# One inference step of a hybrid decoder layer: v as seven block products, one turned buffer, and another order of VectorE's and GpSimd's work around a chunk's norm

## The chip, the cores and the metric

The kernel runs on one core of one Trainium2 chip. The metric is the device time of one execution, in microseconds; the time before is the median of three runs. Everything is float32. Engines are named as in the profile: PE is TensorE, DVE VectorE, ACT ScalarE, POOL GpSimd, SP SyncE, which here only issues DMAs.

## What is computed

One decoder layer for a prompt of 2048 tokens and for 8 sample sequences of 4 tokens, model width 1024.

```python
h = rms_norm(x, norm1_g) * (1 + scale1) + shift1        # shift, scale, gate: silu(c) @ w_ada + b_ada
q, k, v, u, vg = split(h @ w_in)                        # each 512 wide
q, k = rms_norm per head                                # 8 heads of 64
o_sb = stick_breaking(q, k, v)                          # samples: with 8192 past tokens of a paged cache
u = gelu(u); vn = rms_norm(gelu(vg)) per group          # 4 groups of 128
o_mlp = u * (causal w_s @ vn + b_s)                     # in chunks of 128 tokens
x = x + gate1 * (concat(o_sb, o_mlp) @ w_out)
h2 = rms_norm(x, norm2_g) * (1 + scale2) + shift2
up = h2 @ w_up                                          # 5632 wide, then a causal width-3 convolution
x = x + gate2 * ((silu(g_ff) * v_ff) @ w_down)
```

k, v, the samples' vn and the last rows of up are outputs too.

## The kernel before

The program has four stages, each with one instruction list per engine. The engines meet at semaphores alone.

**Preparation** (`prepare`) makes constants and the first third of the conditioning vectors.

**Input projection** (`project_in`) works on pairs of 128-token tiles, 8 pairs, and on one group of the 32 sample rows between pair 6 and pair 7. For u, g, q and k a pair's product [256 x 1024] x [1024 x 512] is split into 2 x 2 blocks and worked as seven block products instead of eight. Their names are 1, 2, 6, 5, 7, 3 and 4; each is four tiles of 128 rows against 256 columns. The differences of weight blocks (`tdiff`) are made once by DVE, and one of them replaces its block in place; the sums of token blocks (`sums`) are made once a pair by POOL. Products 1, 6, 5 and 4 are copied out of PSUM by ACT, 2, 7 and 3 are added by DVE. v is two plain products, one for each tile of tokens: 8 tiles against 512 columns each (line 619). The order of all events is one list, `in_events`, written by hand, which every engine walks through; `with_conditioning` puts into it the steps of the other two thirds of the conditioning product: 16 steps, each one 1024 KB piece of `w_ada` into `ada` and four groups of matmuls with 512 columns side by side (line 650), behind product 5 of u, g, q and k in pairs 1 to 4. Transposed q and k go through the buffer `turned`, the gate's output through `omT`, each copied by ACT (`copy`) and stored by SP. SP issues in the order of the events and waits there, so everything behind a waiting SP instruction waits too.

**Attention of the prompt** (`attend_prompt`) is not changed, but for one small load that is issued in its span, the page table.

**The rest** (`finish_layer`) works on four chunks of 512 tokens, the last with the 32 sample rows. A chunk is a list of units: 4 of the output projection (OUT), 22 of the up projection (UP), 12 of the down projection (DOWN). A unit is again seven block products, in the order 1, (4 of the unit before), 2, 6, 5, 7, 3; the first two UP units are interleaved: 1 1 2 2 5 5 6 3 7 6 4 3 7. Product 6 waits until 1 has been taken out of PSUM, 5 for 2, 7 for 6, 3 for 5 and 4 for 7. POOL makes the sums of a unit's weight blocks one unit ahead (`weight_sums`), DVE the differences of the moving operand (`difference`). Product 5 of an UP unit needs the first difference. The last DOWN unit of a chunk is carried into the next chunk: it stands between that chunk's OUT units and its UP units and covers the norm. The norm: squares (the last four by DVE, line 2124), their sum by PE with a matrix of ones (line 1864), root by ACT, reciprocal by DVE, scaling by DVE and POOL (lines 2169, 2238), modulation by ACT (line 1940), then the four differences for UP (line 2070). In chunk 0 nothing is carried, so the norm has no cover there.

Beside the units runs the attention of the samples over the cache, 64 steps, 23, 22 and 19 of them in chunks 0, 1 and 2. A step is four pieces: SCORE (PE, line 1376; then two sigmoids by ACT), WEIGH (a scan and a product by DVE, lines 1458 and 1462), MOVE (PE transposes, line 1382, and a DVE copy) and SUM (PE, line 1390). Each step needs 8 pages of keys and 8 of values, 256 KB each, that SP loads in order (lines 1334, 1337): the next step's keys when SCORE is done, its values when SUM is done; keys and values have one buffer each. `stage_plan` spreads the pieces: it adds up 1.75 us for each product of a full unit (three quarters of that for the third group of DOWN, nothing for the first two units), places a piece when its share of the chunk's total is due and two products have passed since the last piece, and holds SCORE back from the last OUT unit to the first UP product. In the last 20 us of a chunk's planned cost the two products are not asked for. Before, the first three WEIGHs in chunk 0's UP units stand behind products 31, 39 and 48 of its 258.

Of the kernel before, what the change touches and what calls it, by code (L numbers as in the profile page):

```python
# [12 lines left out]
P = 128  # L13
# [238 lines left out]
def constants(nc, ctx):  # L252

    def sb(name, shape, dt=F32):
# [7 lines left out]
        "bias": sb("bias", [P, 2, H]), "bias_s": sb("bias_s", [P, 2]), "pt": sb("pt", [1, NSEQ * NPAGE], I32),  # L262
# [15 lines left out]
LATE = 2 + NSEQ + 4 * TS  # L278
# [3 lines left out]
def in_events():  # L282
# [7 lines left out]
    for p in groups:  # L290
# [13 lines left out]
        else:  # L304
# [3 lines left out]
        events += [m("u", 1), m("u", 2), *late[0], *once(("tdiff", "g"), m("g", 1), m("g", 2)), m("u", 6), m("u", 5), *late[1], *once(("nsq", SAMPLE, 0)),  # L308
                   m("u", 7), *late[2], m("u", 3)]
        later = lambda *extra: list(extra) if p else []  # L310
        events += [*later(m("g", 1)), m("u", 4), ("gelu", p, "u"), *once(("stat", SAMPLE, 0), ("root", SAMPLE)), *later(m("g", 2)),
# [5 lines left out]
        events += [m("k", 1), m("q", 4), m("k", 2), m("k", 6), ("square", p, "q"), ("reduce", p, "q"), m("k", 5), ("hroot", p, "q"),  # L317
                   m("k", 7), ("hnorm", p, "q"), ("mix", p), *ahead(("modulate",)), m("k", 3), ("om", p)]
        events += [m("v", 0), ("turn", p, "om"), ("copy", p, "om"), *ahead(("sums",)), m("k", 4), ("square", p, "k"), ("reduce", p, "k"), ("turn", p, "q"),
                   ("hroot", p, "k"), ("copy", p, "q"), ("hnorm", p, "k"), ("gain", p, "k"), m("v", 1)]  # L320
# [13 lines left out]

def with_conditioning(events):
# [3 lines left out]
    for event in events:  # L339
# [3 lines left out]
        b = 1 + (n - 1) // KT  # L343
# [7 lines left out]
        if event[1] in range(1, 5) and event[2] in "ugqk" and event[3] == 5:  # L351
            placed.append(("mod", 1 + n // KT, n % KT))
            n += 1
            if n % KT == 0:
                placed.append(("mrow", n // KT))
                since = 0
# [11 lines left out]
def in_bank(p, kind, part):  # L368

    second = part in (2, 5, 3) or (kind == "v" and part == 1)  # L370
    return 2 * (IN_UNITS.index((p, kind)) % 2) + second
# [27 lines left out]
COPIES = [event[1:] + (t,) for event in IN_EVENTS if event[0] == "copy" for t in range(1 if event[1] == SAMPLE else 2)]  # L399
COPY_AT = {turn: n + 1 for n, turn in enumerate(COPIES)}  # L400
# [9 lines left out]
def project_in(nc, sem, a, k, nxt, dr, out):  # L410

    with ExitStack() as ctx:
# [5 lines left out]
        tw = {kind: sb("t_" + kind, [P, 3, halfk, HC]) for kind in "ugqk"}  # L418
        ss = sb("sums", [P, 4, halfk, P])
# [3 lines left out]
        turned, omT = sb("turned", [P, HP, 2 * P]), sb("omT", [P, G, 2 * P])  # L423
# [4 lines left out]
        cT, ada = nxt["cT"], sb("ada", [P, 2 * D])  # L428
# [75 lines left out]
        def _(sp):  # L504
# [21 lines left out]
            def store_cols(use, p):  # L526
# [3 lines left out]
                src, o, first = {"q": (turned, "qT", 0), "k": (turned, "kT", 0), "om": (omT, "catT", DSB)}[use]  # L530
# [4 lines left out]
            def load_ada(b, kt):  # L535
                if kt:
                    sp.wait_ge(mod_done, KT * (b - 1) + kt)
                elif b > 1:
                    sp.wait_ge(mod_turned, b - 1)
                src = a["w_ada"][0].rearrange("(t p) n -> t p n", p=P)[kt][:, 2 * D * b:2 * D * b + 2 * D]  # L540
                sp.dma_start(ada[:], src).then_inc(ada_loaded, 16)
# [14 lines left out]
            late(k["pt"][:], a["page_table"].rearrange("(a b) n -> a (b n)", a=1))  # L556
            for b in range(NSEQ):
                sp.dma_start(k["wd"][TS * b:TS * b + TS, :, TS * b:TS * b + TS], k["wsT"][0:TS, :, 0:TS]).then_inc(nxt["wd_loaded"], 16)
            for event in IN_EVENTS:
                name, *which = event  # L560
                if name == "mul" and which[1:] in (["v", 1], ["g", "s"]):
                    p, kind, part = which
                    if part == 1 and p + 2 < NPAIR:
                        sp.wait_ge(prod_done, prod((p, "v", 1)))
                        load_x(p + 2)
                    sp.wait_ge(taken, IN_TAKEN.index((p, kind, part)) + 1)
# [9 lines left out]
                if name == "mod" and which[1] + 1 < KT:  # L576
# [7 lines left out]
        def _(pe):  # L584
            def multiply(p, kind, part):
# [7 lines left out]
                if part == "s":  # L593
# [5 lines left out]
                    for n, (half, kt) in enumerate(left + right):  # L599
                        first, final = n in (0, KT), n in (KT - 1, KT + len(right) - 1)  # L600
                        into = slice(HC, DSB) if n >= KT else slice(0, HC)
                        for one in many:
                            if one == "v" and n >= KT and half == 0:
                                continue
# [1742 lines left out]
```

## Time and profile before

| | us |
|---|---|
| median of three runs | 3282.31 (3274.2 to 3282.68) |
| the profiled execution's own time | 3281.88 |
| its span | 3280.2 |
| PE busy | 3200.4 |
| DVE, POOL, ACT busy | 1628.4, 1573.4, 1154.9 |

The span is the time from the first instruction to the last in the profiled execution. In a row of the timeline the first number is the start in us from the span's start, the second the time that the merged instructions lasted; a bracket at the end gives the idle time before them and what ended it. The end of a matmul is modelled, so durations of PE are best read from start to start. The input projection lies between about 50 and 585 us, the prompt's attention ends at 1101, and chunks 1, 2 and 3 begin near 1670, 2225 and 2765.

### The profile page before, as it was taken

The page shows a single profiled execution, that of the slowest core. Times are in us where ns is not written, and L with a number is a line of the kernel's source. Part 1 is how long each engine was busy: PE and PEld are TensorE (multiplying, and loading weights), DVE is VectorE, ACT ScalarE, POOL GpSimd, SP SyncE. Part 2 cuts the span into 40 slices and gives each one's busy share as a digit, 9 for nine tenths or more (in the row PEclk, how much of TensorE's full clock was granted, in tenths as well). Part 3 has the DMA queues.
Part 4 walks back from the last instruction along what each step waited for, and adds up shares of the span by engine and source line. Part 5 has one row for each costly group of instructions (what it writes and reads, how often), then busy time and mean ns, then how long its engine had stood idle before and what let it go on. Part 6 is the DMA issues. An engine that isn't in the chain of part 4 may idle for free.

```text
span 3280.2 us, 53057 instructions
## 1 busy us (share of the span) xinstructions
PE 3200.4 (98%) x18534; PEld 2426.1 (74%) x18535; DVE 1628.4 (50%) x2326; ACT 1154.9 (35%) x2436; POOL 1573.4 (48%) x1287
## 2 busy tenths in 40 slices
PE   7999999899999999999999999999999999999999
PEld 5777786666666677777777777777777778788887
DVE  4222222388888554535435544544553445555455
ACT  3333333399999433212103322211331220242221
POOL 2322222176666555545445544544554444476563
PEclk8999999999999999999999999999999999999999
DMA  7233311321312467777886776777777765222222
GB/s 279 84 108 105 109 59 35 81 67 33 69 37 45 161 205 259 244 257 256 280 296 229 241 240 228 251 269 248 251 245 228 245 208 159 68 90 84 84 77 84
DMA packets 260882, 540.93 MB, mean 165 GB/s; under 512 B 45199, under 2 KB 82943, under 8 KB 240137
## 3 DMA queue, kind: packets, MB, share of 16 engines
q1 hardware_dynamic: 225464, 359.31, 34.7%
q10 hardware_dynamic: 35153, 178.23, 15.5%
q8 instruction: 149, 2.44, 0.3%
q14 instruction: 116, 0.95, 0.1%
HBM read 502.90 MB, written 34.55 MB: 164 GB/s over the span
## 4 chain that ended last, share of the span: by engine, by line
PE 60%; DVE 3%; issue 1%; SPq 1%; ACT 0%; DMA 0%; POOL 0%; DVEq 0%; POOLq 0%; ACTq 0%
PE ff_pB L1856 52%; PE s_pZ L1376 4%; PE s_pO L1390 4%; DVE ff_conv L2157 1%; DVE s_left L1458 1%; PE s_pZ L1382 0%; SPq L1326 0%; DVE ff_x L2094 0%; ACT ff_conv L1954 0%; PE s_pZ L1864 0%; DVE ff_raw L2143 0%; SPq L1337 0%; DVE s_stop L1462 0%; DVE ff_act_in L2070 0%; SPq L1334 0%
## 5 line engine op out<-in xcount | busy, mean ns | idle before, releaser
L1856 PE MATMUL ff_pB<-ff_act_in,ff_w 128*128 128x256 f32 (+1 forms) x2496 | 608.5, 388 | 13.4 <-DVE ff_act_in L2070 8.0
L1856 PEld LDWEIGHTS ff_pB<-ff_act_in,ff_w 128*128 128x128 f32 x2496 | 471.9, 192 | 114.3 <-issue 28.8
L2213 POOL TENSOR_TENSOR ff_sums<-ff_w 128x512 f32<-128x512 f32 (+1 forms) x152 | 192.5, 1266 | 729.5 <-PE ff_pB L1856 684.5
L2157 DVE SCALAR_TENSOR_TENSOR ff_conv<-ff_raw,k_vecT,ff_conv 128x512 f32<-128x512 f32 (+1 forms) x352 | 419.1, 1191 | 111.6 <-ACT ff_raw L1961 105.3
L2094 DVE SCALAR_TENSOR_TENSOR ff_x<-ff_pB,k_mod,ff_x 128x256 f32<-128x256 f32 (+2 forms) x448 | 213.9, 479 | 370.6 <-PE ff_pB L1856 368.8
L1856 PE MATMUL ff_pB<-ff_diff_up,ff_sums 128*128 128x256 f32 (+1 forms) x1600 | 388.2, 385 | 2.1 <-DVE ff_x L2094 1.3
L1987 ACT ACTIVATE ff_raw<-ff_pB 128x256 f32<-128x256 f32 (+1 forms) x352 | 135.9, 387 | 720.4 <-PE ff_pB L1856 703.0
L1268 POOL TENSOR_TENSOR at_stop<-at_stop,at_left 128x512 f32<-128x512 f32 (+2 forms) x320 | 314.7, 999 | 151.6 <-ACT at_stop L1203 76.7
L2143 DVE TENSOR_TENSOR ff_raw<-ff_raw,ff_pB 128x256 f32<-128x256 f32 (+1 forms) x264 | 112.0, 425 | 507.6 <-PE ff_pB L1856 507.5
L1856 PEld LDWEIGHTS ff_pB<-ff_diff_up,ff_sums 128*128 128x128 f32 x1600 | 301.2, 190 | 63.5 <-issue 13.6
L1252 DVE TENSOR_TENSOR_SCAN at_left<-at_go,at_left,at_one 128x512 f32<-128x512 f32 x192 | 235.3, 1267 | 47.5 <-ACT at_go L1203 45.2
L1856 PE MATMUL ff_pB<-ff_hidden,ff_w 128*128 128x256 f32 (+1 forms) x1056 | 258.4, 386 | 0.2
L2225 POOL TENSOR_TENSOR ff_raw<-ff_raw,ff_conv 128x512 f32<-128x512 f32 (+1 forms) x88 | 121.1, 1376 | 249.0 <-ACT ff_raw L1967 131.2
L1856 PEld LDWEIGHTS ff_pB<-ff_hidden,ff_w 128*128 128x128 f32 x1056 | 199.2, 191 | 41.1 <-issue 7.9
L2218 POOL TENSOR_TENSOR ff_sums<-ff_w,ff_sums 128x512 f32<-128x512 f32 (+1 forms) x152 | 218.5, 1437 | 11.9
L2216 POOL TENSOR_TENSOR ff_sums<-ff_w 128x512 f32<-128x512 f32 (+1 forms) x152 | 217.9, 1434 | 11.9
L1954 ACT ACTIVATE ff_conv<-ff_raw,k_vecT 128x512 f32<-128x512 f32 (+1 forms) x176 | 145.9, 829 | 209.6 <-DVE ff_raw L2143 207.5
L2214 POOL TENSOR_TENSOR ff_w<-ff_w 128x512 f32<-128x512 f32 (+1 forms) x152 | 206.2, 1356 | 0.0
L1856 PE MATMUL ff_pB<-ff_act_in,ff_sums 128*128 128x256 f32 (+1 forms) x832 | 200.7, 384 | 0.0
L1856 PE MATMUL ff_pB<-ff_diff_down,ff_sums 128*128 128x256 f32 (+1 forms) x768 | 189.3, 390 | 8.3 <-DVE ff_x L2094 7.8
L1856 PE MATMUL ff_pB<-ff_diff_up,ff_w 128*128 128x256 f32 (+1 forms) x800 | 194.1, 385 | 0.0
L1856 PEld LDWEIGHTS ff_pB<-ff_act_in,ff_sums 128*128 128x128 f32 x832 | 156.6, 190 | 31.7 <-issue 8.3
(249 smaller groups left out, 4917.4 us busy)
## 6 DMA issues: line engine op xcount, KB each, us to landing
ff_w<-in_w_units ACTq DMA_DIRECT2D x135, 1024.0 KB, 6.1
s_kpage<-in_cache_k SPq DMA_DIRECT2D x512, 256.0 KB, 3.9
s_vpage<-in_cache_v SPq DMA_DIRECT2D x512, 256.0 KB, 3.3
in_ada<-in_w_ada SPq DMA_DIRECT2D x16, 1024.0 KB, 4.9
ff_w<-in_w_units ACTq DMA_DIRECT2D x16, 768.0 KB, 4.4
in_w<-in_w_in SPq DMA_DIRECT2D x5, 2048.0 KB, 20.7
in_hT<-in_x_cols SPq DMA_DIRECT2D x8, 1024.0 KB, 6.9
wada<-in_w_ada SPq DMA_DIRECT2D x3, 2048.0 KB, 15.5
```

The costliest lines, as they stand in the source:

```text
L1252: dve.tensor_tensor_scan(left[:, e, x0:x1][:, ::-1], go[:, s % RS, e, c0:c1][:, ::-1], other, first, ALU.mult, ALU.bypass).then_inc(left_r ...
L1268: pool.tensor_tensor(w, w, left[:, e, x0 + 1:x1 + 1], ALU.mult).then_inc(w_ready, 1)
L1376: last = pe.matmul(self.pZ[g][32 * sl:32 * sl + 32, 0:ZC].rearrange("p (j t) -> p j t", j=PG), self.q[:, SG * g + sl, hp, :], self.kpage[: ...
L1856: last = pe.matmul(into, left[:, kt * P:(kt + 1) * P], right[:, kt, :], start=kt == 0 and p in (1, 2, 5), stop=kt == depth(n) - 1, skip_gr ...
L1954: act.activation(conv[:, f % 2, half, 0:taps_width(c)], raw[:, f % 2, half, 2:2 + taps_width(c)], ACT.Identity, scale=k["vecT"][:, 196 + f ...
L1987: act.activation(dst, C if p == 5 else A, ACT.Copy).then_inc(taken, 1)
L2094: dve.scalar_tensor_tensor(into, bank[:, 0:hi - lo], mod, into, ALU.mult, ALU.add).then_inc(added, 1)
L2157: dve.scalar_tensor_tensor(cv, raw[:, f % 2, half, i:i + taps_width(c)], tap, cv, ALU.mult, ALU.add).then_inc(tapped, 1)
L2213: pool.tensor_tensor(S3, A11, A21, ALU.subtract).then_inc(sums_ready, 1)
L2214: pool.tensor_tensor(A21, A21, A22, ALU.add).then_inc(sums_ready, 1)
L2216: pool.tensor_tensor(S2, A21, A11, ALU.subtract).then_inc(sums_ready, 1)
L2218: pool.tensor_tensor(S4, A12, S2, ALU.subtract).then_inc(sums_ready, 1)
```

## The change

In the input projection:

- v becomes seven block products like the others, with its own `tdiff` in pair 0; the sample rows add the block that was replaced in place. The order of a pair's events changes: g's products 1 and 2 always stand between u's 2 and 6, v's products are mixed with k's end, and `sums` of the next pair stands behind v's product 7. S1 is made in place of A21, which saves a quarter of `sums`.
- `omT` goes; all copies use `turned`, and each waits for the store of the copy before.
- `ada` is half as large. The conditioning product becomes 32 steps of 512 KB and 256 columns, behind product 5 of all five kinds from pair 1 on.
- The page table's tile moves out of the constants and is loaded among the sample attention's inputs.

In the rest:

- In a chunk with a carried unit, POOL waits for all squares of the norm before it makes the weight sums of the first UP unit. The second half of the sum of squares comes behind the carried unit's product 2 instead of 1.
- The first difference for UP stands behind the second UP unit's product 1 instead of the first UP unit's product 2.
- The samples' scaling in chunk 3 (`scale_sample`) goes from DVE to POOL.
- The planner places a WEIGH only behind a product 7 or 3, and not behind those of the first UP unit, as long as more than 20 us of the chunk's planned cost are left. In chunks 1 and 2 SCORE is held back until the first UP unit's product 5.

```diff
-LATE = 2 + NSEQ + 4 * TS
+LATE = 1 + NSEQ + 4 * TS
...
-        events += [m("v", 0), ("turn", p, "om"), ("copy", p, "om"), *ahead(("sums",)), m("k", 4), ("square", p, "k"), ("reduce", p, "k"), ("turn", p, "q"),
-                   ("hroot", p, "k"), ("copy", p, "q"), ("hnorm", p, "k"), ("gain", p, "k"), m("v", 1)]
+        events += [m("v", 1), m("k", 4), m("v", 2), ("turn", p, "om"), ("copy", p, "om"), ("square", p, "k"), ("reduce", p, "k"), m("v", 6),
+                   ("hroot", p, "k"), m("v", 5), ("hnorm", p, "k"), ("turn", p, "q"), ("copy", p, "q"), ("gain", p, "k"), m("v", 7),
+                   *ahead(("sums",)), m("v", 3), m("v", 4)]
...
+ADA_STEPS = 2 * KT
...
-        if event[1] in range(1, 5) and event[2] in "ugqk" and event[3] == 5:
-            placed.append(("mod", 1 + n // KT, n % KT))
+        if event[1] in range(1, NPAIR) and event[3] == 5 and n < 2 * ADA_STEPS:
+            placed.append(("mod", 1 + n // ADA_STEPS, n % ADA_STEPS))
...
-                        last = pe.matmul(pM[32 * n:32 * n + 32, :], cT[:, kt, :], ada[:, 512 * n:512 * n + 512], start=kt == 0, stop=kt == KT - 1)
+                        last = pe.matmul(pM[32 * n:32 * n + 32, into], cT[:, kt, :], ada[:, 256 * n:256 * n + 256], start=kt == 0, stop=kt == KT - 1)
...
+                    if COPIED_BEFORE[p, use]:
+                        q, other = COPIED_BEFORE[p, use]
+                        act.wait_ge(stored[other], stores(q))
...
-                        pool.wait_ge(prod_done, prod((p - 1, "k", 3)))
-                    pool.tensor_tensor(S1, A21, A22, ALU.add).then_inc(sums_ready, 1)
+                        pool.wait_ge(prod_done, prod((p - 1, "v", 7)))
                     pool.tensor_tensor(S3, A11, A21, ALU.subtract).then_inc(sums_ready, 1)
+                    pool.tensor_tensor(A21, A21, A22, ALU.add).then_inc(sums_ready, 1)
...
-        marks[carried, 1] = roots + [("invert", 0)]
-        marks[carried, 2] = scale(0, 0)
+        marks[carried, 1] = roots[0] + [("invert", 0)]
+        marks[carried, 2] = roots[1] + scale(0, 0)
...
-    for i, place in enumerate(((up, 2), (up + 1, 2), (up, 5), (up + 1, 5))):
+    for i, place in enumerate(((up + 1, 1), (up + 1, 2), (up, 5), (up + 1, 5))):
...
-        if event == ("mul", up, 1):
+        if event == ("mul", up, 5 if c else 1):
             held = False
...
-            if (held and pieces[placed][1] == SCORE) or (since < 2 and total - spent > 20):
+            piece = pieces[placed][1]
+            if (held and piece == SCORE) or (since < 2 and total - spent > 20):
+                break
+            if piece == WEIGH and total - spent > 20 and (event[0] != "mul" or event[2] not in (7, 3) or event[1:] in ((up, 3), (up, 7))):
                 break
...
+                if is_carried(n):
+                    pool.wait_ge(squared_dve, 4 * c + 8)
                 if n + 1 < NU:
                     weight_sums(n + 1)
                 if is_carried(n):
                     scale(c + 1)
```

## Rows read from the trace of the kernel before

**Rows 1.** Busy time and share of TensorE over the span, from the page.
```profile
PE 3200.4 (98%) x18534; PEld 2426.1 (74%) x18535; DVE 1628.4 (50%) x2326; ACT 1154.9 (35%) x2436; POOL 1573.4 (48%) x1287
```

**Rows 2.** Waits of TensorE by what ended them: us in total, times, longest.
```profile
PE ff_pB L1856 <- DVE ff_x L2094: 10.2, 14, 2.2
PE ff_pB L1856 <- DVE ff_act_in L2070: 8.0, 4, 2.9
...
PE s_pZ L1864 <- DVE ff_hidden L2124: 6.1, 4, 3.5
...
PE s_pZ L1376 <- DMA s_kpage<-in_cache_k: 1.9, 2, 1.1
```

**Rows 3.** Timeline of one v product (16 matmuls) and what follows: start, duration, instruction.
```profile
314.20 7.03 PE L619 MATMUL in_pB<-in_w,in_hT 128*128 128x512 f32 x16
...
321.06 1.04 PE L695 MATMUL in_pX<-k_ident,in_raw_u 128*128 128x128 f32 x8
```

**Rows 4.** Timeline of TensorE around one conditioning step in pair 1.
```profile
159.61 1.89 PE L628 MATMUL in_pB<-in_t_k,in_sums 128*128 128x256 f32 x8
161.34 1.89 PE L628 MATMUL in_pB<-in_w,in_sums 128*128 128x256 f32 x8
163.16 1.06 PE L650 MATMUL in_pM<-in_ada,in_cT 128*32 128x512 f32 x8
...
165.98 1.95 PE L678 MATMUL in_pX<-in_raw_g,k_wsT 128*128 128x128 f32 x16
```

**Rows 5.** Timeline of the sample rows' turn of k and its copy.
```profile
574.57 0.43 PE L695 MATMUL in_pX<-k_ident,in_raw_k 32*128 32x32 f32 x4
...
575.39 0.28 ACT L827 ACTIVATE in_turned<-in_pX 128x128 f32<-128x128 f32 x1 [2.03 <-DMA scratch_qT<-in_turned]
```

**Rows 6.** Timeline of TensorE at chunk 0's first product 5 of UP.
```profile
1184.11 3.35 PE L1856 MATMUL ff_pB<-ff_act_in,ff_w 128*128 128x256 f32 x8 [2.16 <-DVE ff_act_in L2070]
...
1187.25 0.63 PE L1382 MATMUL s_pZ<-k_ident,s_stop 128*128 128x128 f32 x2
```

**Rows 7.** Timeline of POOL, DVE and TensorE around chunk 1's norm.
```profile
1727.72 1.27 POOL L2213 TENSOR_TENSOR ff_sums<-ff_w 128x512 f32<-128x512 f32 x1 [6.91 <-PE ff_pB L1856]
1728.13 2.55 DVE L2124 TENSOR_TENSOR ff_hidden<-ff_x 128x256 f32<-128x256 f32 x2
...
1730.73 1.13 PE L1864 MATMUL s_pZ<-ff_hidden,k_ones 128*128 128x256 f32 x4 [1.00 <-DVE ff_hidden L2124]
...
1750.31 1.99 PE L1856 MATMUL ff_pB<-ff_act_in,ff_w 128*128 128x256 f32 x8 [1.49 <-DVE ff_act_in L2070]
```

**Rows 8.** Timeline of TensorE around chunk 3's norm.
```profile
2830.65 2.18 PE L1864 MATMUL s_pZ<-ff_hidden,k_ones 128*128 128x272 f32 x4 [3.54 <-DVE ff_hidden L2124]
...
2832.62 2.77 PE L1856 MATMUL ff_pB<-ff_hidden,ff_w 128*128 128x256 f32 x6
...
2837.20 1.46 PE L1856 MATMUL ff_pB<-ff_hidden,ff_w 128*128 128x256 f32 x6
...
2852.78 5.62 PE L1856 MATMUL ff_pB<-ff_act_in,ff_w 128*128 128x272 f32 x16 [2.91 <-DVE ff_act_in L2070]
```

**Rows 9.** Timeline of TensorE at the first of the long waits on ff_x.
```profile
1385.34 3.20 PE L1856 MATMUL ff_pB<-ff_diff_down,ff_sums 128*128 128x256 f32 x8 [2.10 <-DVE ff_x L2094]
```

**Rows 10.** Timeline of SP's page loads and of two SCOREs, chunks 1 and 2.
```profile
1758.04 9.00 SPq L1337 DMA_DIRECT2D s_vpage<-in_cache_v  x8
...
1780.75 1.93 PE L1376 MATMUL s_pZ<-s_kpage,s_q 128*32 128x256 f32 x32 [1.12 <-DMA s_kpage<-in_cache_k]
...
2315.41 8.38 SPq L1337 DMA_DIRECT2D s_vpage<-in_cache_v  x8
...
2336.93 1.29 PE L1376 MATMUL s_pZ<-s_kpage,s_q 128*32 128x256 f32 x20
```

**Rows 11.** DMA issues: count, KB each, median us from issue to landing.
```profile
s_kpage<-in_cache_k SPq DMA_DIRECT2D x512, 256.0 KB, 3.9
s_vpage<-in_cache_v SPq DMA_DIRECT2D x512, 256.0 KB, 3.3
```

## What was predicted before the run

> **What bounds the kernel now.** I read the busy table first: TensorE works 3200.4 of 3280.2 us [rows 1], so time comes off only by giving it less work or by taking its few waits away. A wait costs it more than its length: after an idle stretch its matmuls run at half pace for some time. Then the waits of TensorE, by what ended them [rows 2]: VectorE's work on the residual tile ff_x (10.2 us), on the operand differences of the up projection (8.0), on the squares of a chunk's norm (6.1); a page of cached keys ended two (1.9). Then the timeline around each place that the diff touches. Everything else that the diff edits lies on engines that wait for TensorE.
>
> **Input projection, v.** A product of 4 tiles of 256 columns starts 1.73 us before the next (159.61 to 161.34) [rows 4]. A v product of before, 8 tiles of 512 columns, takes 6.86 us (314.20 to 321.06) [rows 3], and a pair has two, 13.72. Seven block products take 7 x 1.73 = 12.1. That is 1.62 us less, in 8 pairs: -13.0.
> Beside it: the four subtractions for v stand once, on VectorE in pair 0, where it is mostly idle. ScalarE copies four small blocks and VectorE adds three instead of two large copies. GpSimd's sums for the next pair now start after v's product 7 and have v's 3 and 4, u's 1 and 2, the turn of k and g's 1 and 2 before their first user, six products or 10.4 us, for three operations that last 1.3 us each; that is what moving g's two products ahead covers. I cost all of these at nothing; one miss on TensorE would cost 1 to 3 us in each pair.
>
> **The conditioning product in 32 halves.** It sits between two products: 161.34 to 165.98 is 4.64 us, two products are 3.45, so one step costs 1.19 us [rows 4]. Its two passes of 512 columns take 2 x 0.429 (6.86 us / 16 matmuls), four groups side by side; the other 0.33 us is the change over. With 256 columns: 0.43 + 0.33 = 0.76. 32 x 0.76 - 16 x 1.19 = +5.3. The ends are 0 (cost halves with the columns) and +19 (cost stays); I take +5.3. The loads are half as large and the closest two steps are 5 products apart.
>
> **One turned buffer.** Each copy now waits for the store of the copy before. For a full pair some 4 us of products lie between om's copy and q's, and more before k's. For the sample rows they follow at once: before, the copy of k waited 2.03 us for q's store and stood at 575.39, while TensorE's turn of k was at 574.57 [rows 5]. Now om's copy waits for that store, and the turn of k needs om's bank back: 575.4 + 0.3 - 574.6 = +1.1. The page table's load moves behind other loads; nothing needs it for 500 us.
> Input projection: -13.0 + 5.3 + 1.1 = -6.6.
>
> **The norms, one per chunk.** Chunk 0: VectorE's first difference stood behind a sample step's scan and VectorE's add, TensorE idled 2.16 us and the next product took 3.14 instead of 1.73 (1184.11 to 1187.25) [rows 6]. Now the difference is one product earlier and the scan (WEIGH) can't stand in the block: 2.16 + 1.41 = -3.6. The idle time ahead of the block, which waits for the norm itself, stays.
> Chunks 1 and 2: two squares took 2.55 us (1728.13) [rows 7], where one alone takes 0.42, beside GpSimd's weight sums of 1.27 us each. Now GpSimd waits for all squares and the second half's sum comes one product later: the wait of 1.00 goes, and a wait of 0.4 behind it. The wait for the difference, 1.49, shrinks to about 0.4, since the scores and the scan leave, but the modulated tiles come no sooner. -2.4 each, -4.8.
> Chunk 3: 3.54 us of waiting, 1.1 in the slow sum and, from 2832.62 to 2837.20, 4.58 us for what takes 2.6 [rows 8]: 6.6. At the difference 2.91 idle, and 5.62 for two products that at 1.83 and a tail of 0.16 take 3.8: 4.7. The three sample operations leave VectorE for GpSimd and end about when ScalarE's last modulation does; I leave 0.5. -10.8.
> On the slow squares the Trainium skill, "SBUF — State Buffer", section "Who interferes with whom", says that GpSimd and a VectorE operation with two SBUF inputs exclude each other for a whole instruction. By that rule the trace agrees (1.27 us a square beside sums of 1.27 us), and it speaks against the change too: GpSimd's later sums meet the differences.
> GpSimd's next sums end 0.5 to 1.5 us later than before; they are needed three products on. Norms: -19.2.
>
> **WEIGH only behind products 7 and 3.** Of the 14 waits on ff_x [rows 2], 11 with 8.3 us fall where sample steps run, the longest with a scan ahead of the add that product 5 needs, and then the product takes 3.20 instead of 1.89 [rows 9]; that happens twice. 8.3 + 2.6 = 10.9 at most. Behind 3 the scan meets the taps, so I take -9.
>
> **What the rule costs.** The planner spreads pieces by time and asks for two products between them. A step is SCORE, WEIGH, MOVE, SUM. In a unit the order is 1, 4, 2, 6, 5, 7, 3. When the planner is late, a WEIGH behind 7 is followed by MOVE +2, SUM +4, SCORE +6 and WEIGH +8, behind the next unit's 3; from a 3, +8 is forbidden and the next is +13. So two steps cost at least 21 products, 10.5 each. Chunk 0 has 418.25 us of planned cost for 23 steps, or 10.4 products each: it can't catch up. Its first WEIGH in the block of up units moves from product 31 to 40, and the next ones, worked on, are at 48, 61, 69, 82 and so on to 237. At product 243 the remaining cost falls to 19.7 and the rule lapses (it holds above 20); 84 pieces are placed and 87.7 are due, so SCORE, WEIGH, MOVE and SUM of one step stand at one place. Chunks 1 and 2 need only 11.8 and 12.1 products a step and catch up near products 240 and 200.
> The bunch: let S be the start of the SUM before it, two small products (2.6 us) and that SUM (1.9) earlier than the SCORE. Its values are issued at S+2.1, in 8 to 9 us (1758.04) [rows 10], and land 3.3 later [rows 11]: S+13.5. Without waiting TensorE would be there at S+6.6, after SCORE and MOVE: +7. The next keys are issued after the values: S+2.1+8.2+0.8+8.2+3.9 = S+23.2, and that SCORE would be reached at S+18 to 19: +4.5. Half pace after both: +2.5. Together +14. Ends: +5 (only the scan's latency) and +19.
> Late steps also crowd the pages. 25 times (9 in chunk 0, 9, 7) a SCORE is 10 products behind the SUM that lets SP start on 16 page loads. Before this spacing occurs three times: 1.12 us of waiting (1780.75) [rows 10], 0.8, and none (2336.93) [rows 10]. In the last 21.5 us lie between the first issue (2315.41) and the SCORE; needed are two sets of issues of 8.2 to 9 each, 0.8 between them and 3.9 to land [rows 11], 21.1 to 22.7. 25 x 0.35 = +9; ends 0 and +28.
>
> **The sum.** -6.6 - 19.2 - 9 + 14 + 9 = -11.8 on the profiled execution's own 3281.88 us, 3270.1; the median of before is 0.4 above it: 3270.5.
>
> **Rivals.**
> A, the gains without the crowding: SP's loads land in time everywhere and the bunch costs its scan's latency alone (+5). Speaks for it: the loads take 0.74 to 0.77 of the DMA engines, not all, and the case in chunk 2 has no wait. Against: two of three waited. 3282.3 - 34.8 + 5 = 3252.5.
> B, the other side: pages become the bound. Each late SCORE waits the 1.12 us of the longer case (+28), and the bunch costs +19, against gains of 34.8: +12, 3294.5. It decides against the change from 0.64 us a place on, with a bunch of 19, which is just the mean of the three waits; for 1.12 speaks that both waits fell where a weight load ran beside, against it that after a step of 13 products SP has nothing left over.
> C, GpSimd becomes late at the norms and in the differences: its sums of 1.3 us, held back until the squares are done, meet VectorE's four differences in each of four blocks and hold product 5 or 6 by 1.3 to 2.5 us with half pace behind. The norms then give 8 instead of 19: 3281. For it: GpSimd has no idle time in the block; against: its sums are needed later than the differences. The lock of the skill's page gives the same, with each difference 1.3 us later.
>
> **Numbers.** Forecast 0.45 (its own range 3262 to 3280), A 0.2, B 0.1, C 0.2, the rest 0.05. The range is 3250 to 3289. About 0.3%, 9.8 us, is what a measurement can tell from no change, so faster means below 3272.5. Of the forecast 0.6 lies below, all of A, nothing of B, 0.15 of C: faster 0.5. Slower, above 3292: 0.09. The same: 0.41.
>
> **What would show it.** Matmuls into in_pB with 512 columns gone, v's products 1.73 apart, and the conditioning matmuls 64 x 4 with 256 columns, no waits of TensorE among them: right. The stretch to the end of the input projection shorter by 6 to 7 us. Waits on ff_hidden's squares near 0.5 us in total, on differences below 1.5. Waits of s_pZ for s_kpage of some 13 us, over 20 times, and one for s_vpage of over 2 near the end of chunk 0, with MOVE directly behind SCORE. If neither is there, A holds; if keys wait over 25 us, B; if the sums stand as releasers of product 5 or 6, C. A new wait in the input projection would refute my zeros there.

## The result, and the profile after

| | before | after |
|---|---|---|
| median of 6 runs, us | 3282.49 (3274.2 to 3284.04) | 3299.05 (3295.49 to 3305.3) |
| span of the profiled execution | 3280.2 | 3303.3 |

The ratio is 1.0061 with a 95% interval of 1.005 to 1.0072: slower by 0.6%, which is more than the 0.3% that a measurement can tell from no change. "After" is the changed kernel. The forecast was 3270.5 (range 3250 to 3289, 0.09 for slower). It was wrong in sign.

From the profile of after, its busy line and the chain of work that ended last. In before that chain was 60% PE and 1% SPq, SP's own instructions:

```profile
PE 3197.2 (97%) x18862; PEld 2465.7 (75%) x18863; DVE 1648.0 (50%) x2351; ACT 1156.4 (35%) x2452; POOL 1593.9 (48%) x1290
...
PE 47%; SPq 8%; DVE 4%; issue 4%; DMA 3%; ACT 1%; POOL 0%; DVEq 0%; ACTq 0%; POOLq 0%
```

PE works 3 us less than in [rows 1] and the span is 23 us longer, so some 26 us of new idle time stand somewhere. The waits of PE in after, by what ended them, in the form of [rows 2] (us in total, times, longest):

```profile
PE s_pZ L1375 <- DMA s_kpage<-in_cache_k: 22.2, 19, 2.4
PE s_pO L1389 <- DVE s_wT L1465: 13.7, 11, 2.9
PE ff_pB L1859 <- DVE ff_x L2097: 11.5, 17, 1.7
...
PE s_pO L1389 <- DMA s_vpage<-in_cache_v: 4.3, 1, 4.3
...
PE in_pX L696 <- ACT in_turned L822: 3.2, 1, 3.2
...
PE s_pZ L1867 <- DVE ff_hidden L2127: 0.5, 1, 0.5
```

Keys were expected (some 13 us, over 20 times), the one wait for values of over 2 too, and the squares at 0.5. Two lines were not: SUM waits 13.7 us for s_wT, the copy of the moved weights, and ff_x has as much as in [rows 2] where I had taken 9 us off.

To see where the time lies I cut each trace at the first matmul of a norm's sum of squares (us; a stage runs from one chunk's norm to the next, the last to the end of the span):

| kernel | chunk 0's norm to 1's | to 2's | to 3's | to the end |
|---|---|---|---|---|
| before | 562.4 | 557.4 | 539.7 | 460.0 |
| after | 588.9 | 563.2 | 542.9 | 450.7 |
| norms_alone | 557.5 | 554.9 | 538.1 | 450.4 |
| no_rule | 557.1 | 554.9 | 538.1 | 450.7 |
| half_pages | 579.1 | 558.2 | 540.7 | 450.7 |
| move_act | 583.8 | 558.9 | 539.2 | 450.7 |
| half_move | 570.8 | 555.1 | 536.6 | 450.7 |
| late_only | 557.0 | 566.0 | 542.7 | 450.7 |

The last column, where no sample step runs, has most of the gain that was worked out (9.3 of 10.8). The loss stands where sample steps run, most of it in chunk 0. The other kernels of the table are the experiments.

### The profile page after: what moved, and what is told of

Its sections match the earlier page's. It is cut to its first block, busy times and chain, and to the rows that moved or that the text cites. A ratio compares the mean times of both kernels' runs of the same rounds, so it can differ in the third digit from the quotient of the medians.

```text
span 3303.3 us, 53814 instructions
## 1 busy us (share of the span) xinstructions
PE 3197.2 (97%) x18862; PEld 2465.7 (75%) x18863; DVE 1648.0 (50%) x2351; ACT 1156.4 (35%) x2452; POOL 1593.9 (48%) x1290
## 4 chain that ended last, share of the span: by engine, by line
PE 47%; SPq 8%; DVE 4%; issue 4%; DMA 3%; ACT 1%; POOL 0%; DVEq 0%; ACTq 0%; POOLq 0%
PE ff_pB L1859 41%; SPq L1325 4%; DMA s_kpage<-in_cache_k 3%; PE s_pO L1389 3%; PE s_pZ L1375 3%; DVE ff_conv L2160 2%; SPq L1336 2%; SPq L1333 2%; ACT ff_conv L1957 1%; DVE ff_act_in L2172 0%; DVE ff_x L2097 0%; DVE s_left L1457 0%; DVE ff_raw L2146 0%; DVE ff_diff_down L2073 0%; PE s_pZ L1867 0%
## 5 line engine op out<-in xcount | busy, mean ns | idle before, releaser
L1859 PEld LDWEIGHTS ff_pB<-ff_act_in,ff_w 128*128 128x128 f32 x2496 | 471.7, 191 | 96.6 <-issue 22.2
L628 PE MATMUL in_pB<-in_w,in_hT 128*128 128x256 f32 x960 | 229.7, 386 | 6.0 <-ACT in_hT L782 6.0
L2204 POOL TENSOR_TENSOR ff_w<-ff_w 128x512 f32<-128x512 f32 (+1 forms) x152 | 216.1, 1422 | 0.0
L628 PEld LDWEIGHTS in_pB<-in_w,in_hT 128*128 128x128 f32 x960 | 185.4, 194 | 32.9 <-issue 6.6
```

The costliest lines, as they stand in the source:

```text
L628: last = pe.matmul(bank[:, 0:HC], left[:, kt, :], right[:, kt, :], start=kt == 0 and part in (1, 2, 5), stop=kt == halfk - 1, skip_group_c ...
L1859: last = pe.matmul(into, left[:, kt * P:(kt + 1) * P], right[:, kt, :], start=kt == 0 and p in (1, 2, 5), stop=kt == depth(n) - 1, skip_gr ...
L2204: pool.tensor_tensor(A21, A21, A22, ALU.add).then_inc(sums_ready, 1)
```

## The experiments

All times are medians. The kernel before ran beside each on the same chip, and the ratio is to that. Kernels of different tables are best compared by their ratios.

### One part of the change at a time

**input_alone** takes the input projection (and the page table's move), **norms_alone** the other order around the norm, **rule_alone** the planner's rule on WEIGH. Each is the kernel before with the lines of the change for that part. **no_rule** is the changed kernel without the rule:

```diff
-            if piece == WEIGH and total - spent > 20 and (event[0] != "mul" or event[2] not in (7, 3) or event[1:] in ((up, 3), (up, 7))):
-                break
```

> The kernel before with the input projection of the changed one (v as seven products, conditioning in halves, one turned buffer, the page table's move) and nothing else of the change. Theory (the two traces: the first product of the last stage starts 2.1 us earlier, since 7.6 us are gained up to the sample rows and most of it is lost again around their stores): 2 us less than before, about 3280.5. Rival (the working of the prediction): 6.6 us less, 3276. Second rival: the input projection is what made the changed kernel slower, by something its own trace hides behind the later stages; then over 3290.

> The kernel before with only the other order around a chunk's norm (GpSimd waits for all squares, the second half's root one product later, the first difference one product earlier, scores held back to product 5, the sample rows' scaling on GpSimd). Theory (chunk 3's norm took 9.3 us less in the changed kernel's trace, chunk 0's block 3 to 4, chunks 1 and 2 about 1 to 2.4 each): 14 to 19 us less than before, about 3266. Rival (GpSimd's later weight sums meet VectorE's differences and hold products 5 or 6): 8 us or less, 3275 or more.

> The kernel before with only the planner's rule that a WEIGH stands behind a product 7 or 3. Theory (the rule makes steps late in each chunk; pages of keys, the SUM behind VectorE's copy of the moved weights, and the bunch at the end of chunk 0 then hold TensorE): 30 to 36 us more than before, about 3315, with over 15 waits on s_kpage. Rival (the rule costs no more than it saves, and what slowed the changed kernel is the input projection's or the norms'): 3274 to 3290.

> The changed kernel without the planner's rule on WEIGH, all else kept. Theory: the rule alone made it slower, so this one is faster than both, 3262 to 3268, with fewer than 5 waits on s_kpage and the waits of SUM on s_wT gone. Rival (pages wait for another reason, such as the input projection's or the norms' shift): 3295 to 3300, the waits on s_kpage stay.

| kernel | us | ratio | 95% interval |
|---|---|---|---|
| before, in the same runs | 3280.54 | | |
| input_alone | 3276.87 | 0.9987 | 0.9978 to 0.9996 |
| norms_alone | 3263.52 | 0.9946 | 0.9932 to 0.9959 |
| rule_alone | 3311.10 | 1.0090 | 1.0077 to 1.0104 |
| no_rule | 3263.31 | 0.9941 | 0.9928 to 0.9955 |

The rule alone costs 30.6 us on before, and in the changed kernel 0.0120 of 3281, 39 us. It is the whole of the loss: without it the changed kernel is 17 us faster than before. Part of the 9 us between the two prices is that on before the rule also does some of the norms' work: rule_alone's waits on the first differences are 3.7 us where before has 8.0 [rows 2]. The norms give 17.0; norms_alone's stages in the table are shorter than before's by 4.9, 2.5, 1.6 and 9.6, together 18.5. The input projection gives 3.7 with an interval of 1.3 to 7.2, so the 2.1 of the two traces and the 6.6 of the prediction both lie in it, and this run doesn't decide between them.

The waits of rule_alone and, below it, of no_rule, which has none of a SCORE on s_kpage and none of a SUM of the steps on s_wT. Those two lines come with the rule and go with it. The rule takes nothing from ff_x in total: the two longest waits there, 2.10 and 2.19 us, are gone in after, and three of 1.67 have come.

```profile
PE s_pZ L1376 <- DMA s_kpage<-in_cache_k: 19.3, 17, 2.2
PE s_pO L1390 <- DVE s_wT L1466: 11.5, 11, 2.9
PE ff_pB L1859 <- DVE ff_x L2097: 10.6, 15, 1.7
```

```profile
PE ff_pB L1857 <- DVE ff_x L2095: 11.3, 16, 2.2
...
PE s_pZ L1381 <- DVE s_stop L1461: 4.5, 6, 0.9
```

### What the rule's price is made of

**half_pages** loads half of each page and lets it stand in for the other half, so that it leaves out half of the cached keys and values but keeps TensorE's work; **move_act** moves one copy from VectorE to ScalarE, **half_move** does both, all in the changed kernel.

```diff
-                sp.dma_start(self.kpage[:, j, sl, :], src).then_inc(self.k_loaded, 16)
+                sp.dma_start(self.kpage[:, j, sl, 0:DSB // 2], src[:, 0:DSB // 2]).then_inc(self.k_loaded, 16)
```

```diff
 def act_piece(self, act, N, i):
...
+        if i == MOVE:
+            act.wait_ge(self.wT_done, N + 3)
+            act.activation(self.wT[:].rearrange("p j q -> p (j q)"), self.pZ[g][:, ZC:ZC + PG * P], ACT.Copy).then_inc(self.wT_read, 1)
...
 def dve_piece(self, dve, N, i):
...
-        if i == MOVE:
-            dve.wait_ge(self.wT_done, N + 3)
-            self.dve_move(dve, slice(0, P), PG, g)
```

> The changed kernel with page loads of half the size: of each cached page only the first 256 of 512 columns are loaded and stand in for the other 256 too (so half of the cached keys and values is left out), TensorE's matmuls keep their number and size. Theory (late steps let SP's page loads, bound by their data, end the waits: 22.2 us on keys and 4.3 on values in the changed kernel's trace, plus some half pace behind them): 22 to 30 us less, 3269 to 3277, no waits on s_kpage, the 13.7 us of SUM on s_wT stay. Rival (SP's own work of issuing, not the data, sets the pace): eight loads still take over 6 us to issue, over 10 us of waits on s_kpage stay, over 3285.

> The changed kernel with the copy of the moved weights (s_wT) on ScalarE instead of VectorE, so that it doesn't queue behind VectorE's taps. Theory: the 11 waits of SUM, 13.7 us, go, with some half pace behind them: 14 to 18 us less, 3281 to 3285. Rival (pages set the pace of the steps whatever SUM does): the waits on s_kpage grow by as much and the time stays over 3293.

> Both edits, half-size page loads and the copy on ScalarE, in the changed kernel. Theory (pages and the late copy are all that the planner's rule costs): 3255 to 3263, at or below the kernel without the rule (3263.3); below it if the rule does take away collisions of the scan with the adds. Rival (a further cost of late steps that neither edit touches): over 3268.

| kernel | us | ratio | 95% interval |
|---|---|---|---|
| before, in the same runs | 3280.97 | | |
| half_pages | 3285.34 | 1.0014 | 1.0005 to 1.0023 |
| move_act | 3289.76 | 1.0025 | 1.0015 to 1.0034 |
| half_move | 3273.68 | 0.9976 | 0.9967 to 0.9985 |

Against the changed kernel's ratio the three are 15, 12 and 28 us faster. All three forecasts missed: I had 22 to 30 for half_pages, which came out at its rival's edge, 14 to 18 for move_act, and half_move at or below no_rule, where it stays 11 us above by the ratios.

move_act's waits show that the two causes hang together, and that the copy was not freed altogether:

```profile
PE s_pZ L1375 <- DMA s_kpage<-in_cache_k: 15.3, 16, 3.0
PE ff_pB L1859 <- DVE ff_x L2097: 13.9, 21, 1.7
...
PE s_pO L1389 <- ACT s_wT L1422: 5.6, 4, 1.8
```

SUM's wait falls from 13.7 to 5.6 us, the waits for keys fall with it by 6.9, although no load was changed, and ff_x rises by 2.4. A SUM that is late delays the loads behind it. So the price of the late copy and that of the pages can't be added up singly.

The stages say where the rest lies. Of the 45 us by which after's first three stages are longer than no_rule's, the two edits together take 32.5. In chunks 1 and 2 half_move is within 0.2 of no_rule and 1.5 below it; the two waits are all that the rule costs there. In chunk 0 it stays 13.8 above. Laid against no_rule matmul by matmul, it is 1.8 us ahead at 1620 us, 13.8 behind at 1654 and 13.8 behind at the chunk's end. So what is left arises in that one place, near the end of chunk 0, where SCORE, WEIGH, MOVE and SUM of one step stand behind one product. The matmuls of PE there, start, duration, what it idled for:

```profile
1637.87 0.44 PE L1381 MATMUL s_pZ<-k_ident,s_stop 128*128 128x128 f32 x2 [1.91 <-DVE s_stop L1465]
1643.43 3.64 PE L1390 MATMUL s_pO<-s_vpage,s_wT 128*32 128x512 f32 x16 [5.13 <-DMA s_vpage<-in_cache_v]
```

The same place in the changed kernel, with SP's loads:

```profile
1646.54 1.92 PE L1389 MATMUL s_pO<-s_vpage,s_wT 128*32 128x512 f32 x16
...
1648.72 8.40 SPq L1336 DMA_DIRECT2D s_vpage<-in_cache_v  x8
...
1652.81 1.93 PE L1375 MATMUL s_pZ<-s_kpage,s_q 128*32 128x256 f32 x32 [1.56 <-DMA s_kpage<-in_cache_k]
...
1656.64 0.44 PE L1381 MATMUL s_pZ<-k_ident,s_stop 128*128 128x128 f32 x2 [1.90 <-DVE s_stop L1461]
...
1661.35 3.64 PE L1389 MATMUL s_pO<-s_vpage,s_wT 128*32 128x512 f32 x16 [4.27 <-DMA s_vpage<-in_cache_v]
1664.92 2.50 PE L1859 MATMUL ff_pB<-ff_hidden,ff_sums 128*128 128x256 f32 x6
```

With S = 1646.54 the values are issued at S+2.2 and the SUM starts at S+14.8; the prediction had S+2.1 and S+13.5. Idle 1.56, 1.90 and 4.27, then 1.7 and 1.0 of half pace, and 0.35 and 1.21 at the next two SCOREs (1669.07 and 1693.43): 12.0, where I had put 14. Three of these waits, 3.1 us, are among the 22.2 us for keys. No run takes the bunch away by itself.

half_pages also shows what paces the page loads. The timeline of SP in half_pages, one set of keys and one of values:

```profile
1209.52 8.39 SPq L1333 DMA_DIRECT2D s_kpage<-in_cache_k  x8
1219.00 8.15 SPq L1336 DMA_DIRECT2D s_vpage<-in_cache_v  x8
```

and in the changed kernel:

```profile
1211.50 8.40 SPq L1333 DMA_DIRECT2D s_kpage<-in_cache_k  x8
1220.71 8.04 SPq L1336 DMA_DIRECT2D s_vpage<-in_cache_v  x8
```

The DMA issues (KB each, median us from issue to landing) of half_pages and then of the changed kernel, where [rows 11] had 3.9:

```profile
s_kpage<-in_cache_k SPq DMA_DIRECT2D x512, 128.0 KB, 2.6
```

```profile
s_kpage<-in_cache_k SPq DMA_DIRECT2D x512, 256.0 KB, 4.6
```

Half the bytes leave the eight issues at 8.0 to 8.4 us. The bytes don't set that pace, as the rival said; SP's own instructions fill most of it. What fell is the landing, by 2.0 us, and since the mean wait on keys was 22.2 / 19 = 1.17, that was enough: of 22.2 us 2.9 stayed, in one wait behind the bunch. So the rival was right about the pace, and the theory about the waits. By the instructions of the address lookup, from the trace of the changed kernel (duration min/median/max in ns), a load takes 269 + 152 ns ahead of its issue, which itself takes 338; from one load to the next it is 1.1 us:

```profile
L1325 SPq TENSOR_LOAD <-k_pt x32: 262/269/287, 1202.8 to 1237.9; - x32
L1325 SPq FUSED_REGOPS  x32: 152/152/159, 1203.1 to 1238.5; - x32
```

**late_only** keeps the rule in chunks 1 and 2 alone:

```diff
-            if piece == WEIGH and total - spent > 20 and (event[0] != "mul" ...
+            if c and piece == WEIGH and total - spent > 20 and (event[0] != "mul" ...
```

> The changed kernel with the planner's rule on WEIGH in chunks 1 and 2 only; chunk 0 is planned without it. Theory (chunk 0, whose steps can't catch up and end in the bunch, pays 32 of the rule's 45 us in the traces, chunk 1 8 and chunk 2 5): 10 to 16 us above the kernel without the rule, 3272 to 3279. Rival (chunks 1 and 2 catch up as chunk 0 can't, and their waits are the run's own spread): within 4 us of 3263.

It took 3274.51 us (before 3280.37), ratio 0.998, interval 0.997 to 0.9989: 11 us above no_rule by the medians and 13 by the ratios, as the theory had it. Chunk 0 is back at 557.0. So chunk 0 pays about 32 of the rule's 45 us in the traces, by the table. Chunk 1 is 2.8 us longer here than in after (566.0 against 563.2) under the same rule; why, I did not find.

### The sample rows' stores

**no_rule_cols** is no_rule with three separate places in the one turned buffer for the 32 sample rows:

```diff
+SAMPLE_COLUMN = {"q": 0, "om": S, "k": 2 * S}
...
-                    if COPIED_BEFORE[p, use]:
+                    at = SAMPLE_COLUMN[use] if p == SAMPLE else 0
+                    if at == 0 and COPIED_BEFORE[p, use]:
...
-                        into = dst[:, :, t * R:(t + 1) * R]
+                        into = dst[:, :, at + t * R:at + (t + 1) * R]
```

> The changed kernel without the planner's rule, and with the three stores of the sample rows' turned tiles taken from columns of their own (0, 32 and 64) of the one turned buffer, so that their copies don't wait for one another's stores. Theory (the copy of om waited 4.3 us for a store queued behind a conditioning load; TensorE then idled 2.7 to 3.2 us and ran at half pace for some 3 more): 4 to 6 us less than without the columns, 3257 to 3260, the wait on in_turned gone. Rival (TensorE's turns wait for something else in its place, or the store of q then holds the conditioning step): 3261 to 3265.

It took 3256.47 us, ratio 0.9920 (0.9907 to 0.9934): 6.8 us less than no_rule, a little more than the 4 to 6 of the theory. What it took away, in the changed kernel:

```profile
569.66 0.40 SPq L547 DMA_DIRECT2D in_ada<-in_w_ada  x1
...
570.47 0.38 SPq L537 DMA_DIRECT2D scratch_qT<-in_turned  x1
574.72 0.28 ACT L822 ACTIVATE in_turned<-in_pX 128x128 f32<-128x128 f32 x1 [4.28 <-DMA scratch_qT<-in_turned]
...
575.14 0.60 PE L696 MATMUL in_pX<-k_ident,in_raw_k 32*128 32x32 f32 x4 [3.24 <-ACT in_turned L822]
575.67 3.78 PE L628 MATMUL in_pB<-in_w,in_sums 128*128 128x256 f32 x8
```

and in no_rule_cols:

```profile
571.25 0.43 PE L698 MATMUL in_pX<-k_ident,in_raw_k 32*128 32x32 f32 x4
571.61 1.99 PE L630 MATMUL in_pB<-in_w,in_sums 128*128 128x256 f32 x8
```

The store of q took 4.2 us to land where it had taken 2.2 before. SP had issued a 512 KB conditioning load 0.8 us ahead of it, which itself took 4.7. That the load is the cause is read from this order; no run moves the load alone, and no_rule_cols takes away the wait and not the slow landing. The Trainium skill, "DMA: Bandwidth & Descriptors", section "Queues, rings and completion order", says that each DMA engine works off the descriptors of one issuing engine in ring order; by that rule the trace agrees, the store landing 0.35 us behind the load.

### Two gentler rules

**narrow** is no_rule_cols with a WEIGH forbidden only behind product 6; **narrow3** adds a third product between WEIGH and MOVE in chunks 1 and 2; **move3** has only that.

```diff
+            if piece == WEIGH and total - spent > 20 and event[0] == "mul" and event[2] == 6:
+                break
+            if piece == MOVE and c and since < 3:
+                break
```

> The changed kernel with columns of their own for the sample rows' stores, and in place of the rule on WEIGH a narrow one: no WEIGH directly behind a product 6, the only place where a scan ran into the add that product 5's successor needs for over 2 us (twice, with under 1 us in other places). Theory: the steps keep their spacing, two waits of 2.1 and 2.2 us on ff_x go, with some slow matmuls behind: 3 to 6 us less than with the columns alone (3256.5), so 3250 to 3253. Rival (a WEIGH one product later meets the taps, and the wait only moves to SUM or MOVE): 3255 to 3258.

> As the kernel with the narrow rule, and in chunks 1 and 2 a MOVE stands at least three products behind its WEIGH instead of two. Theory (MOVE waited five times 0.8 to 0.9 us for the weights in the trace without the rule): 3 to 5 us less than the narrow rule alone. Rival (each step's SUM comes a product later, and the pages of keys after it become late, as under the full rule): no gain, or up to 5 us more, with waits on s_kpage.

> As no_rule_cols (no rule on WEIGH, columns of their own for the sample rows), and in chunks 1 and 2 a MOVE stands at least three products behind its WEIGH; the narrow rule of the run before is left out. Theory (the gain of that run over the narrow rule came from MOVE no longer waiting behind the taps and the scan, and the narrow rule itself gave nothing): 3250 to 3254, no waits on s_stop in chunks 1 and 2. Rival (both are needed, since only a WEIGH off product 6 avoids the two long waits on ff_x): 3255 to 3260.

| kernel | us | before beside it | ratio | 95% interval |
|---|---|---|---|---|
| narrow | 3265.06 | 3280.37 | 0.9956 | 0.9943 to 0.9970 |
| narrow3 | 3252.14 | 3280.37 | 0.9912 | 0.9899 to 0.9926 |
| move3 | 3257.13 | 3281.22 | 0.9924 | 0.9911 to 0.9938 |

narrow was a miss of 12 us or more, on the side of its rival and beyond it. Its stages are 2.4 and 3.3 us longer than no_rule_cols's in chunks 1 and 2. Its trace has MOVE waiting 3.73 us, in chunk 1 and again in chunk 2, because the scan, one product later, came behind the taps and ran at 1.85 us instead of 0.75, beside a GpSimd operation (1764.08, 1.26 us):

```profile
1760.42 3.51 DVE L2163 SCALAR_TENSOR_TENSOR ff_conv<-ff_raw,k_vecT,ff_conv 128x512 f32<-128x512 f32 x2
...
1764.03 1.85 DVE L1460 TENSOR_TENSOR_SCAN s_left<-s_go,s_left 128x256 f32<-128x256 f32 x1
...
1767.11 0.44 PE L1384 MATMUL s_pZ<-k_ident,s_stop 128*128 128x128 f32 x2 [3.73 <-DVE s_stop L1464]
```

narrow3 has none of these waits. It is the fastest kernel of the study, 29 us (0.88%) below before and 49 below the changed one by the ratios, and 14 below narrow, where I had forecast 3 to 5. move3 missed its 3250 to 3254 and came out in its rival's range: MOVE still waits three times in it, 4.9 us in all. narrow3's gain over no_rule_cols (0.9912 against 0.9920) and move3's lack of one lie inside the intervals, so whether its two edits help, and which, stays open; ff_x keeps 10.9 us of waits in it.

## Why the prediction was wrong

Step by step, on the traces of before and after; the terms of the prediction sum to -11.8, the spans differ by +23.1. The medians differ by 16.6; the profiled execution of after is the slowest of its six, 6.3 us above their median.

| term | predicted | measured | by |
|---|---|---|---|
| input projection | -6.6 | -2.1 | start of the first OUT product |
| norms | -19.2 | -18.5 | stages, norms_alone |
| WEIGH out of the adds' way | -9 | 0 | ff_x: 11.3 us in no_rule, 11.5 in after |
| bunch at product 243 | +14 | 12 to 14 | rows above; half_move's chunk 0 |
| waits for keys | +9 | 17 | stages, half_pages against after |
| SUM waiting for s_wT | not foreseen | 13 | stages, move_act against after |

The last three rows overlap (three waits for keys stand in the bunch, and the waits for keys shrink in move_act), so the column is no exact sum.

**The step that failed is the price of the rule.** I had -9 + 14 + 9 = +14 for it, it is 39 by the ratios (45 by the traces of after and no_rule). The -9 did not come, the +9 for pages was half of what they cost, and the wait of SUM for VectorE's copy was not in the sum at all. Only the bunch was sized right.

- *The collisions.* I took the scan ahead of product 5's add as gone, and allowed 1.9 us for the rest: "Behind 3 the scan meets the taps, so I take -9." That half sentence was the whole point. Taps are two instructions of 0.75 to 1.9 us each, and what queues behind them now is the add that the next product needs. In after, the scan at product 3, then the taps, then the add, on DVE, and the product that waited:

```profile
1402.24 1.41 DVE L1457 TENSOR_TENSOR_SCAN s_left<-s_go,s_left 128x256 f32<-128x256 f32 x1
...
1404.92 3.43 DVE L2160 SCALAR_TENSOR_TENSOR ff_conv<-ff_raw,k_vecT,ff_conv 128x512 f32<-128x512 f32 x2
...
1408.27 0.47 DVE L2097 SCALAR_TENSOR_TENSOR ff_x<-ff_pB,k_mod,ff_x 128x256 f32<-128x256 f32 x1
...
1408.89 1.97 PE L1859 MATMUL ff_pB<-ff_diff_down,ff_sums 128*128 128x256 f32 x8 [1.67 <-DVE ff_x L2097]
```

- *The piece behind the piece.* I placed WEIGH with care and let MOVE and SUM follow at +2 and +4 products without asking what their DVE part meets. Pinning WEIGH to 7 and 3 pins MOVE too, and its copy then stands behind the taps of the unit before, here behind a difference too. SUM waits for it, four times by 2.85 or 2.86 us:

```profile
1337.13 2.28 DVE L2073 TENSOR_TENSOR ff_diff_down<-ff_hidden,ff_diff_down 128x1024 f32<-128x1024 f32 x1
...
1340.80 2.43 DVE L2160 SCALAR_TENSOR_TENSOR ff_conv<-ff_raw,k_vecT,ff_conv 128x512 f32<-128x512 f32 x2 [1.05 <-ACT ff_raw L1964]
...
1343.54 0.42 DVE L1465 COPY s_wT<-s_pZ 128x256 f32<-128x256 f32 x1
...
1344.01 1.92 PE L1389 MATMUL s_pO<-s_vpage,s_wT 128*32 128x512 f32 x16 [2.86 <-DVE s_wT L1465]
```

- *The keys.* The mechanism was right, the count and the size were not. In the changed kernel's order a SCORE of the late steps stands 10 products behind that SUM 19 times outside the bunch (9, 6 and 4 in chunks 0, 1 and 2), not 25 times (9, 9 and 7); the last such place is at product 167 of chunk 1 and 125 of chunk 2, so they catch up earlier than I had it. 16 of the 19 wait, 19.1 us together, 1.00 a place where I had 0.35; the other three of the 19 waits stand at the bunch and behind it. I had formed 0.35 from a spread of 21.1 to 22.7 against 21.5 and let the case without a wait [rows 10] weigh too much. Rival B's 1.12 a place was near. The landing also grew, from 3.9 to 4.6 in the median, which no term had.
- *Rival B* gave 3294.5 and the time was 3299.05. Its mechanism, late steps that wait for pages, is shown, but it is not all, and its number is partly luck: it had 28 us at 25 places where 19.1 were waited at 19, and half_pages leaves three fifths of the rule's price. Rival A is out by the waits for keys. C is out as a price: no weight sum of GpSimd stands as releaser of product 5 or 6, and the norms gave what was forecast. The meeting that it rests on is there: in chunk 1 the second and third of the first differences last 1.63 and 2.19 us where they took 1.22 in before, but TensorE has no wait on a difference in after.

**The input projection** was right up to the sample rows: v's products stand 1.73 apart, PE reaches the sample rows' product for k at 540.93 instead of 548.57, 7.6 us earlier. By then 7 of the 8 pairs and 30 of the 32 conditioning steps are done (the last pair runs behind the sample rows, to 632 us in both traces and not to about 585), for which the prediction's own prices give -11.34 + 3.76 = -7.58. Two products with a conditioning step between them take from 583.78 to 588.00, 4.22 us, 0.77 more than two plain ones, as predicted (0.76). The term that was mis-sized is the sample rows' wait: 1.1 us worked out from the store's old landing time, 6 to 7 measured (no_rule_cols: 6.8): the store now stood behind a conditioning load, and half pace followed. The gain at the first OUT product also differs between traces with the same input projection, 2.1 us in after, 2.7 in no_rule and 3.7 in input_alone.

**The norms** were right in sum and within 1.3 us in each of the four places (-4.9, -2.5, -1.6, -9.6 against -3.6, -2.4, -2.4, -10.8). Some of that is chance: the products behind the two long waits on ff_x, in the stages of chunk 0 and chunk 2, ran 1.2 and 1.1 us faster in norms_alone than in before, though nothing was changed there (see the last section). The squares of the norm no longer meet GpSimd: one takes 0.42 us, and GpSimd's sum starts 0.1 us behind the last.

```profile
1749.78 0.42 DVE L2127 TENSOR_TENSOR ff_hidden<-ff_x 128x256 f32<-128x256 f32 x1
...
1751.51 0.76 DVE L2127 TENSOR_TENSOR ff_hidden<-ff_x 128x256 f32<-128x256 f32 x2
...
1752.35 1.27 POOL L2203 TENSOR_TENSOR ff_sums<-ff_w 128x512 f32<-128x512 f32 x1 [10.20 <-DVE ff_hidden L2127]
```

My opening sentence that a wait costs TensorE more than its length was right of some waits and not of others of the same length (see the last section).

What stays open: the ratios put the rule's price at 39 us and the traces at 45; the changed kernel's own runs spread over 10 us, 3295.5 to 3305.3, and with one trace of it I can't say which waits differ from run to run. The page loads were not made faster to issue, and the bunch was read from traces and not taken away by itself.

## What to carry to other kernels

When a rule confines one piece of a chain to certain slots, follow every later piece of the chain into its new slot and ask what each of its engine's instructions stands behind there; here the piece that was placed with care gained nothing, and its successors, the page loads behind them and the bunch cost 39 us. Where a stream of small transfers has a fixed period of issue, compare that period and the landing with the shortest spacing of its users, count the places in the planner's output, and take the longest wait already seen as the price of each further such spacing. A shared buffer with a wait for its last store is as slow as what is queued ahead of that store.

## What the runs showed of the hardware that was not expected

- **The pace of the page loads is that of SP's instructions, not of bytes.** 8.0 to 8.4 us for eight loads of 256 KB and of 128 KB alike, 1.1 us from one to the next, of which the address lookup (421 ns) is more than the issue instruction (338 ns). The bytes only set the landing: 4.6 and 2.6 us for keys.
- **The same wait was followed by half the clock in one execution and not in another.** Nine of the kernels have a wait of 2.10 us on ff_x at the same product. That product took 1.99 us in five of them (norms_alone, no_rule, narrow3, move3, late_only) and 2.81 to 3.55 in four (before [rows 9], input_alone, no_rule_cols, narrow). In no_rule and in narrow:

```profile
1378.68 1.99 PE L1857 MATMUL ff_pB<-ff_diff_down,ff_sums 128*128 128x256 f32 x8 [2.10 <-DVE ff_x L2095]
```

```profile
1371.80 2.81 PE L1862 MATMUL ff_pB<-ff_diff_down,ff_sums 128*128 128x256 f32 x8 [2.10 <-DVE ff_x L2100]
```

Of narrow's two waits of 3.73 us one left the next product at 1.89 us, behind the other it took 3.17. The SCOREs behind after's 19 waits for keys, 0.35 to 2.40 us long, all took 1.93 us as those without a wait. So the half pace behind a wait of 2.1 to 3.7 us is a term that comes and goes, 1 us or more each time, and a difference of that size between two traces shows nothing about the edit.
- **Four SUMs of after stand behind waits of 2.85 or 2.86 us.** One took 1.92 us, the others 2.40, 3.18 and 3.52. The granted clock over 2 us of the one that took 1.92 and over 3.5 us of the one that took 3.52 (columns: us, PE busy, granted clock, DMA share, GB/s), and below them the bunch's SUM behind 4.27 us, which ran at half the clock, so at 1.2 GHz of 2.4:

```profile
1344.00:1346.00 2.00, 1.99 (x17) 1.00 0.95 389
...
1533.90:1537.40 3.50, 3.50 (x17) 0.54 0.63 262
...
1661.40:1665.00 3.60, 3.60 (x17) 0.50 0.81 244
```
